# Two attention loops: scores of two key groups issued in alternating pairs, two score tiles in each slot

## The reference

```python
# first block: 16 heads of 64, 2 key/value groups of 8 heads, blocks of 128 queries
kb, vb = with_prev(k), with_prev(v)                     # key block n-1 and n
s = einsum('bnqkgd,bnskd->bnkgqs', q, kb) * HD ** -0.5
logits = where(mask, s - slopes * dist, NEG)
m = maximum(max(logits), sink)
p = exp(logits - m)
probs = p / (sum(p) + exp(sink - m))
o = einsum('bnkgqs,bnskd->bnqkgd', probs, vb)
...
# second block: 8 heads of 64, 2 key/value groups of 4 heads
s_win = where(valid, einsum('bnqhgd,bnkhd->bnhgqk', qb, kw) * scale, NEG_INF)  # blocks n-1, n, n+1
s_ctx = einsum('bnqhgd,bchd->bnhgqc', qb, kc) * scale                         # 256 context keys
p_win, p_ctx = _sink_softmax([s_win, s_ctx], sink)
o = einsum('bnhgqk,bnkhd->bnqhgd', p_win, vw) + einsum('bnhgqc,bchd->bnqhgd', p_ctx, vc)
```

## Time and profile before

| what | value |
|---|---|
| time, median of 3 runs | 2345.18 us (2345.18 to 2348.38) |
| the profiled execution | 2351.11 us, its span on the core 2349.1 us |
| PE / DVE / ACT / POOL busy | 92% / 54% / 31% / 30% of the span |
| `swa` attention | from 149 us to 330 us of the span |
| `win` attention | from 2044 us to 2232 us of the span |

### The profile page before, as it was taken

How to read it: one execution, slowest core, us unless ns; L and a number is a source line. 1 busy time by engine, 2 the same in 40 slices (tenths; PEclk the granted TensorE clock), 3 DMA queues, 4 the chain that set the end, 5 groups by cost and what they waited for, 6 DMA issues and landing times. The chain is left out here.

```text
span 2349.1 us, 29236 instructions
## 1 busy us (share of the span) xinstructions
PE 2171.5 (92%) x10132; PEld 1766.1 (75%) x10132; DVE 1264.1 (54%) x1972; ACT 728.0 (31%) x1358; POOL 700.5 (30%) x359
## 2 busy tenths in 40 slices
PE   4999989999999999999889889979989999979896
PEld 3876668788888888888578778668867788766675
DVE  6137852672371371473669999785252122378724
ACT  4236542421221220222442122432152211156522
POOL 4223322322222222222244762142132222234422
PEclk9987889899999999999899989989999999979998
DMA  4100021231231231231201012124121211100031
GB/s 137 67 27 1 1 89 46 81 127 52 72 134 45 76 129 45 89 116 49 113 27 36 29 66 82 56 75 177 36 111 45 81 45 53 45 5 14 10 116 72
DMA packets 42690, 157.16 MB, mean 67 GB/s; under 512 B 4224, under 2 KB 8960, under 8 KB 41344
## 3 DMA queue, kind: packets, MB, share of 16 engines
q1 hardware_dynamic: 40176, 146.49, 17.9%
q10 hardware_dynamic: 2448, 9.84, 1.1%
HBM read 136.39 MB, written 19.92 MB: 67 GB/s over the span
## 5 line engine op out<-in xcount | busy, mean ns | idle before, releaser
L161 POOL TENSOR_TENSOR wL<-wst,wH 128x1024 fp32r<-128x1024 f32 x139 | 360.3, 2592 | 1139.8 <-ACT wH L156 1139.5
L190 PE MATMUL banks<-u2H,wH 128*128 128x512 f32 x736 | 295.7, 402 | 29.4 <-POOL wL L161 18.6
L191 PE MATMUL banks<-u2L,wH 128*128 128x512 f32 x736 | 291.5, 396 | 0.0
L192 PE MATMUL banks<-u2H,wL 128*128 128x512 f32 x736 | 291.1, 396 | 0.0
L190 PE MATMUL banks<-uH,wH 128*128 128x512 f32 x672 | 262.7, 391 | 2.0 <-DVE uL L387 1.5
L191 PE MATMUL banks<-uL,wH 128*128 128x512 f32 x672 | 262.2, 390 | 0.0
L192 PE MATMUL banks<-uH,wL 128*128 128x512 f32 x672 | 262.2, 390 | 0.0
L1298 DVE SCALAR_TENSOR_TENSOR conv_out<-conv_in,par,conv_out x120 | 242.1, 2018 | 21.6 <-DVE conv_out L1298 20.9
L190 PE MATMUL banks<-aH,wH 128*128 128x512 f32 x640 | 249.9, 390 | 2.2 <-PEq L213 2.2
L191 PE MATMUL banks<-aL,wH 128*128 128x512 f32 x640 | 249.5, 390 | 0.0
L192 PE MATMUL banks<-aH,wL 128*128 128x512 f32 x640 | 249.5, 390 | 0.0
(11 more groups left out here) (279 smaller groups left out, 4012.0 us busy)
## 6 DMA issues: line engine op xcount, KB each, us to landing
wst<-in_wstream SPq DMA_DIRECT2D x153, 512.0 KB, 3.3
mod_w<-in_mod_w SPq DMA_DIRECT2D x48, 512.0 KB, 6.0
x_scratch<-h SPq DMA_DIRECT2D x2, 4096.0 KB, 11.8
gt<-gates_scratch SPq DMA_DIRECT2D x8, 640.0 KB, 4.0
h<-in_x SPq DMA_DIRECT2D x4, 1024.0 KB, 10.7
h<-in_x SPq DMA_DIRECT2D x1, 4096.0 KB, 12.1
h<-x_scratch SPq DMA_DIRECT2D x1, 4096.0 KB, 12.2
xo<-x_scratch SPq DMA_DIRECT2D x1, 4096.0 KB, 12.2
```

The lines of the kernel that those rows point to most:

```text
L161: pool.tensor_tensor(wL[:, slot, :], wst[:, slot, :], wH[:, slot, :].bitcast(F32), ALU.subtract)\
L190: first = pe.matmul(out, aH, bH, start=start, stop=False)
L191: pe.matmul(out, aH, bL, start=False, stop=False)
L192: return first, pe.matmul(out, aL, bH, start=False, stop=stop)
```

## The change

Three edits in `attention`.

1. The plan: `a_slot = 2`, `extra = 0` for all steps. A full step of `swa` now has the tiles {0,1}, {2,3}, {}, {}; one of `win` {0,1}, {2,3}, {4,5}, {6,7}, {8,9}, {10,11} in slots 0 to 5.
2. `score` makes two tiles at a time, one of each group, and their matmuls alternate: high x high of kv=0, the same of kv=1, high x low of kv=0, of kv=1, and so on. The number of matmuls, their shapes and the two signals `s_done` stay.
3. Before, tile g waited until tile g-3 had been read out of its bank. Now the pair g, g+1 waits before its first matmul until tile g-2 has been read, which the pair's second tile needs.

```diff
-                a_slot = 1 if ns <= nt else 2
+                a_slot = 2
...
-                extra = 1 if nt else 0
+                extra = 0
...
                         g = sidx[k] + x
-                        if g >= S_RING:
-                            pe.wait_ge(s_free, g - S_RING + 1)
+                        if g + 1 >= S_RING:
+                            pe.wait_ge(s_free, g + 1 - S_RING + 1)
                         n, cg = steps[k]
-                        for y, (hs, kv, c, col, w, off, boff) in enumerate(s_tiles(steps[k])[x]):
...
-                            _, m = mm3(pe, banks[:, g % S_RING, boff:boff + w], QH[rows, c, q], QL[rows, c, q],
-                                       KH[rows, col:col + w], KL[rows, col:col + w], True, True)
-                        m.then_inc(s_done, 1)
+                        q = slice(n * P, n * P + P)
+                        both = [s_tiles(steps[k])[x + kv] for kv in range(2)]
+                        for y in range(len(both[0])):
+                            for part in range(3):
+                                for kv in range(2):
+                                    hs, kv_, c, col, w, off, boff = both[kv][y]
+                                    assert kv_ == kv
+                                    rows = slice(64 * kv, 64 * kv + 64)
+                                    m = pe.matmul(banks[:, (g + kv) % S_RING, boff:boff + w], (QL if part == 2 else QH)[rows, c, q],
+                                                  (KL if part == 1 else KH)[rows, col:col + w], start=part == 0, stop=part == 2)
+                                    if part == 2 and y == len(both[0]) - 1:
+                                        m.then_inc(s_done, 1)
...
-                        for y in slot.scores:
+                        for y in slot.scores[::2]:
```

More of the change, by code:

```diff
@@ L674, in score @@
                         g = sidx[k] + x
-                        if g >= S_RING:
-                            pe.wait_ge(s_free, g - S_RING + 1)
+                        if g + 1 >= S_RING:
+                            pe.wait_ge(s_free, g + 1 - S_RING + 1)
                         n, cg = steps[k]
-                        for y, (hs, kv, c, col, w, off, boff) in enumerate(s_tiles(steps[k])[x]):
-                            rows = slice(64 * kv, 64 * kv + 64)
-                            q = slice(n * P, n * P + P)
-                            _, m = mm3(pe, banks[:, g % S_RING, boff:boff + w], QH[rows, c, q], QL[rows, c, q],
-                                       KH[rows, col:col + w], KL[rows, col:col + w], True, True)
-                        m.then_inc(s_done, 1)
+                        q = slice(n * P, n * P + P)
[10 more added lines that the diff above has]
+                                        m.then_inc(s_done, 1)
                     def turn(k, x):
```

## The result

The changed kernel takes 2356.98 us (median of six runs, 2355.14 to 2359.25) against 2346.64 us of the kernel before, run beside it (2345.18 to 2350.46, six runs). The ratio is 1.0042, with a 95% interval of 1.0029 to 1.0055: slower by about 10 us. The forecast was 2354 and slower. The profiled execution took 2359.25 us with a span of 2357.2, 8.1 more than the span before. I measure each attention from its first score matmul to the first matmul of the next stage, and its steps from the end of one `neg_max` to the end of the next: `swa` went from 181.6 to 179.5 us and `win` from 190.4 to 200.6. The rest of the program is unchanged, and the two terms, -2.1 and +10.2, are the whole difference between the two profiles.

The account below looks back on a forecast made before the run. The program was taken as PE's, but in both attentions PE and DVE hand work to each other and their waits count. Full and first steps: `swa` -2 and +1, `win` +6 and +4, sum +9 us, 2354 us; range 2337 to 2367.

Follow-up runs that it names:

- e7: Kernel before, with five throwaway matmuls added before the first turn of each `swa` step from step 2 on; 2332.2 us, ratio 0.9929.
- e8: Changed kernel with the same slots, pairs and pair waits, but the two tiles' matmuls following one another instead of alternating; 2366.5 us.
- e9: Changed kernel's new slots alone, each tile issued by itself and waiting only for its own bank; 2350.6 us.
- e10: e7 with throwaway matmuls added in the waits of the first steps, 22 in `swa` and 20 in `win`; 2334.3 us, ratio 0.9936.

## What to carry to other kernels

An order that lets TensorE do the same work in less time can lose if it must wait for two buffers at once: look at what the ring of buffers allows before pairing. Where TensorE's work gets less and its granted clock doesn't rise, the saved time has turned into waiting. Such a wait can be filled, with useful work or else with throwaway matmuls, but they must end when the wait ends.

## What the runs showed of the hardware

- Matmuls that compute nothing made the kernel 17 us faster (e7: 70 of them; the clock in the full steps of `swa` went from 0.80 to 1.00).
- The length of the wait alone doesn't tell whether the clock falls. Waits of 2.87 us in the changed kernel were followed by half clock at 2158.6 and not after 2136.3; in e8 the clock stayed at 1.00 over 82 us with waits of 2.06 to 2.09 us in every step, and in e9 it fell behind waits of 1.85. What decides it stays open.

The stretch of e8, with PE busy 75% of it:

```profile
194.00:276.00 82.00, 61.84 (x416) 47.70 (x416) 70.35 (x233) 53.25 (x176) 30.50 (x33) 1.00 0.00 1
```

- PE can be busy nearly all the time and the clock stay down: in e10 it was busy 16.78 of 17.00 us at half clock, most of it with the score matmuls of 64 rows (25.5 us of overlapping records against 6.2 of other matmuls). Why was not tried.
- Two score tiles of different row groups that stand side by side overlap in part even when they are issued one after the other: 1.26 us for a pair, against 0.90 in alternation.
